# Expert loop of a transformer kernel: one split of both units of a load in place of two

## The reference

```python
def swiglu(h, w_gate, w_up, w_down):
    return (jax.nn.silu(h @ w_gate) * (h @ w_up)) @ w_down

def moe_swiglu(h, router, w_gate, w_up, w_down):
    ...
    probs = jax.nn.softmax((ht @ router).astype(jnp.float32), axis=-1)
    vals, idx = lax.top_k(probs, TOP_K)
    wts = vals / jnp.sum(vals, axis=-1, keepdims=True)
    gates = jnp.einsum('tk,tke->te', wts, jax.nn.one_hot(idx, N_EXPERTS, dtype=jnp.float32)).astype(h.dtype)
    for e in range(N_EXPERTS):
        out = out + gates[:, e:e + 1] * swiglu(ht, w_gate[e], w_up[e], w_down[e])
    return out.reshape(bsz, seq, d)
```

## Time and profile before

| what | us |
|---|---|
| median of 3 runs | 1398.68 |
| lowest, highest | 1397.64, 1400.05 |
| the profiled execution | 1395.94 |
| its span, first to last instruction | 1393.9 |
| TensorE busy in the span | 1306.4 |
| VectorE busy | 1045.1 |
| ScalarE busy | 864.5 |

### The profile page before, as it was taken

The page is one execution under the profiler, slowest core; times in us unless marked ns, Lnnn a source line. Parts: engine busy times, 40 slices in busy tenths (PEclk is TensorE's granted clock), DMA queues, the critical chain, the costliest instruction groups (busy, mean ns, idle before and its releaser), DMA issues.

```text
span 1393.9 us, 18776 instructions
## 1 busy us (share of the span) xinstructions
PE 1306.4 (94%) x6058; PEld 1067.9 (77%) x6058; DVE 1045.1 (75%) x1471; ACT 864.5 (62%) x1272; POOL 38.9 (3%) x54
## 2 busy tenths in 40 slices
PE   7999999997678999999999999999997975999998
PEld 5878888886556788888888888888886744888887
DVE  4576555565765999999999999999995856555554
ACT  4655444455644687878787878878784544444443
POOL 0000000000300000000000000000000111000000
PEclk9999999998898999999999999999998997999999
DMA  9635555554004597979798888889894410445540
GB/s 359 218 147 199 190 185 181 182 180 151 31 10 172 207 377 303 379 295 382 299 380 327 354 331 344 329 347 366 319 375 157 168 44 1 136 185 193 181 151 31
DMA packets 46121, 319.31 MB, mean 229 GB/s; under 512 B 5152, under 2 KB 6304, under 8 KB 7808
## 3 DMA queue, kind: packets, MB, share of 16 engines
q1 hardware_dynamic: 44288, 316.40, 60.1%
q10 hardware_dynamic: 1680, 2.10, 0.5%
q0 software_dynamic: 112, 0.26, 0.1%
HBM read 316.64 MB, written 2.10 MB: 229 GB/s over the span
## 4 chain that ended last, share of the span: by engine, by line
PE 81%; DVE 11%; issue 3%; ACT 2%; POOL 1%; DMA 1%; DVEq 0%; SPq 0%; ACTq 0%; POOLq 0%
PE bank L349 24%; PE bank L351 24%; PE bank L350 24%; PE bank L645 3%; DVE wl L1231 2%; PE bank L413 2%; DVE x L1645 2%; PE bank L385 1%; DMA fixed<-fixed_dram 1%; PE bank L751 1%; PE bank L580 0%; PE bank L772 0%; PE bank L664 0%; PE bank L665 0%; DVE xtl L1251 0%
## 5 line engine op out<-in xcount | busy, mean ns | idle before, releaser
L1231 DVE TENSOR_TENSOR wl<-raw,wh 128x1024 fp32r<-128x1024 f32 x598 | 714.8, 1221 | 206.0 <-ACT wh L835 194.3
L835 ACT ACTIVATE wh<-raw 128x1024 fp32r<-128x1024 f32 x598 | 631.5, 1061 | 323.1 <-PE bank L351 316.2
L349 PE MATMUL bank<-wh,xth 128*128 128x512 f32 (+2 forms) x1170 | 463.4, 396 | 12.9 <-DVE wl L1231 5.1
L351 PE MATMUL bank<-wh,xtl 128*128 128x512 f32 (+2 forms) x1170 | 454.6, 389 | 0.0
L350 PE MATMUL bank<-wl,xth 128*128 128x512 f32 (+2 forms) x1170 | 454.5, 388 | 0.0
L349 PEld LDWEIGHTS bank<-wh,xth 128*128 128x128 f32 x1170 | 221.5, 189 | 57.8 <-issue 5.3
L351 PEld LDWEIGHTS bank<-wh,xtl 128*128 128x128 f32 x1170 | 221.2, 189 | 46.0
L350 PEld LDWEIGHTS bank<-wl,xth 128*128 128x128 f32 x1170 | 221.8, 190 | 42.3
L349 PE MATMUL bank<-wh,hth 128*128 128x512 f32 x456 | 178.6, 392 | 0.0
L351 PE MATMUL bank<-wh,htl 128*128 128x512 f32 x456 | 178.0, 390 | 0.0
L350 PE MATMUL bank<-wl,hth 128*128 128x512 f32 x456 | 177.4, 389 | 0.0
(11 more groups left out here) (275 smaller groups left out, 794.2 us busy)
## 6 DMA issues: line engine op xcount, KB each, us to landing
raw<-weights_dram SPq DMA_DIRECT2D x299, 1024.0 KB, 4.9
x<-x_dram SPq DMA_DIRECT2D x1, 1024.0 KB, 7.9
bias_scratch<-act ACTq DMA_DIRECT2D x1, 1024.0 KB, 16.0
wide<-bias_scratch ACTq DMA_DIRECT2D x8, 128.0 KB, 2.2
out_dram<-x SPq DMA_DIRECT2D x4, 256.0 KB, 2.1
fixed<-fixed_dram SPq DMA_DIRECT2D x1, 600.0 KB, 8.9
rows<-rows_dram POOLq DMA_DIRECT2D x1, 256.0 KB, 6.3
cols<-cols_dram SPq DMA_DIRECT2D x1, 73.0 KB, 8.6
```

Of the source, the lines that this page charges most:

```text
L349: mm(o, lh, wh[:, wi, sl], start=start, stop=False)
L351: return mm(o, ll, wh[:, wi, sl], start=False, stop=stop)
L835: A(wh[:, c % SPLIT, :], raw[:, (c // 2) % RAW, (c % 2) * UNIT:(c % 2 + 1) * UNIT], ACT.Copy).then_inc(hi_done, 1)
L1231: V.tensor_tensor(wl[:, c % SPLIT, :], raw[:, (c // 2) % RAW, (c % 2) * UNIT:(c % 2 + 1) * UNIT], f32(wh[:, c % SPLIT, :]), ALU.subtract). ...
```

## The change

In the expert loop alone (`nt` is 1 there, and 2 in the dense layers, which keep the old functions) `follow` and `followed` are replaced by `follow_pairs` and `followed_pairs` on ScalarE and on VectorE. One instruction splits both units of a load, 2048 columns. ScalarE's waits until both slots are free, and `followed_pairs` does n - 2 units ahead of its step and 2 behind, where `followed` did n - 1 and 1. The number of slots, the loads and TensorE's program stay as they were. In the diff the lines of ScalarE are shown, and of VectorE those that differ from them; its `ffn` has the same replacements.

```diff
+            def split_hi_pair(c, i):
+
+                sc.wait_ge(raw_full[(c // 2) % RAW], 16 * (c // ROUND + 1) + 16 * i)
+                sc.wait_ge(unit_used, c - SPLIT + 2 + ROUND * i)
+                A(wh[:, c % SPLIT:c % SPLIT + 2, :], raw[:, (c // 2) % RAW, :].rearrange("p (u n) -> p u n", u=2), ACT.Copy)\
+                    .then_inc(hi_done, 2)
+
+            def follow_pairs(c, n, i):
+
+                for u in range(c, c + n, 2):
+                    split_hi_pair(u + SPLIT, i)
+
+            def followed_pairs(c, n, i, step):
+
+                follow_pairs(c, n - 2, i)
+                sc.wait_ge(unit_used, c + n + ROUND * i)
+                step()
+                follow_pairs(c + n - 2, 2, i)
+
...
             def ffn(tag, c0, nf, U, loops, width, nd, i0, f0=0, nt=NT, early=None, late=None, done=0, leave=None):
                 nj = width // P
+                some, most = (follow, followed) if nt == NT else (follow_pairs, followed_pairs)
...
-                followed(c0, ug, i0, lambda: evac(0, fb))
+                most(c0, ug, i0, lambda: evac(0, fb))
...
-                    followed(c0 + ug, ug, i0, lambda: evac(1, fb))
-                follow(c0 + 2 * ug, nd, i0)
+                    most(c0 + ug, ug, i0, lambda: evac(1, fb))
+                some(c0 + 2 * ug, nd, i0)
...
-                        followed(c + s * (ug + nd), ug, ii, lambda: evac(2 + s, fb + it * U))
-                        follow(c + s * (ug + nd) + ug, nd, ii)
+                        most(c + s * (ug + nd), ug, ii, lambda: evac(2 + s, fb + it * U))
+                        some(c + s * (ug + nd) + ug, nd, ii)
                         turned(2 + s, fb + it * U)
...
                 if late:
                     late[0]()
-                    followed(c, nd, i0, late[1])
+                    most(c, nd, i0, late[1])
...
+            def split_lo_pair(c, i):
+                dv.wait_ge(hi_done, c + 2 + ROUND * i)
+                V.tensor_tensor(wl[:, c % SPLIT:c % SPLIT + 2, :], raw[:, (c // 2) % RAW, :].rearrange("p (u n) -> p u n", u=2),
+                                f32(wh[:, c % SPLIT:c % SPLIT + 2, :]), ALU.subtract).then_inc(lo_done, 2)
+
+            def follow_pairs(c, n, i):
+                for u in range(c, c + n, 2):
+                    split_lo_pair(u + SPLIT, i)
+
+            def followed_pairs(c, n, i, step):
+
+                follow_pairs(c, n - 2, i)
+                step()
+                follow_pairs(c + n - 2, 2, i)
+
```

More of the change, by code:

```diff
@@ L900, in ffn @@
                 fb = nf * f0
-                followed(c0, ug, i0, lambda: evac(0, fb))
+                most(c0, ug, i0, lambda: evac(0, fb))
                 if nt == NT:
-                    follow(c0 + ug, 2, 0)
+                    some(c0 + ug, 2, 0)
                     turned(0, fb)
-                    followed(c0 + ug + 2, 2, 0, lambda: evac(1, fb, 6))
+                    most(c0 + ug + 2, 2, 0, lambda: evac(1, fb, 6))
                 else:
@@ L920, in ffn @@
                 for f in range(2 + loops * U, nf):
-                    followed(c, ug, i0, lambda: evac(f, fb))
+                    most(c, ug, i0, lambda: evac(f, fb))
                     if nt == NT and f == nf - 1:
                         turned(f, fb, True)
-                        follow(c + ug, nd, i0)
+                        some(c + ug, nd, i0)
                     else:
-                        follow(c + ug, nd, i0)
+                        some(c + ug, nd, i0)
                         turned(f, fb)
```

## The result

The changed kernel takes 1426.24 us (median of 4 runs, 1423.73 to 1427.65) against 1399.37 us before (4 runs, 1397.64 to 1402.27): a ratio of 1.0186, 95% interval 1.0171 to 1.0202. Run again beside 20 runs of the kernel before on another occasion it took 1425.34 against 1400.76 us, 1.0186 (1.0164 to 1.0208). The forecast was 1413.2 us, with a range of 1403 to 1430.

A forecast was written before the change was run, and what follows sets the result against it. TensorE was taken to set the pace, so the change could mainly lose cover. 8 x 1.09 + 7 x 0.55 + 1.90 = 14.5 us on 1398.68 gave 1413.2 us, range 1403 to 1430.

The forecast's parts named there:

- What bounds it: Expert loop: TensorE sets the pace in a steady stage; the change can gain little and can lose cover.
- Prices: Time of one pair split: 1.91 us on ScalarE, 2.28 us on VectorE.
- Late: End of an expert: the pair delays htl for the down product behind the gather, 1.09 us in each of 8 experts.
- Early: Start of the next expert: hbuf's first turn waits 0.69 us more; 0.55 us net, counted for 7 experts.
- End of the loop: Behind the last expert: the last additions to x wait behind the last pair, 1.90 us once.
- Steady stage: Stages within an expert: cover ahead of hbuf's turn shrinks from 0.73 to 0.18 us but holds, so cost nothing.
- longer steady stages: Expert loop: steady stages were to stay at 8.4 us; if they lengthen, the forecast is wrong.
- the dearer case: Rival, pairs at twice the single price: steady stages 0.19 us short, 1432 us in all; chance of 1421 and more 0.18.
- the dear ones: Upper end of the pair prices, twice the single: 2.12 us on ScalarE, 2.44 us on VectorE.
- The faster one: Rival: VectorE's relief removes TensorE's waits at the turns, 8 x 0.55 = 4.4 us, giving 1394.3 us; chance 0.05.
- the no-change rival: Rival: late pair behind the gather costs under 0.3 us an expert, less the 4.4 us gain; about 1398; chance 0.06.
- the forecast proper: Whole kernel: a time of 1407 to 1421 us, given chance 0.60.

The follow-up runs named there:

- e8: Changed kernel with ScalarE's program put back to singles in the old order, VectorE still in pairs: period 73.88 us, ratio 1.0007 to the kernel before.
- e9: Changed kernel with ScalarE's old program and the turned hbuf written ahead of the last splits on both engines: period 73.56 us, ratio 1.0006 to the kernel before.
- e2: Changed kernel with the turned hbuf written ahead of the last pair in every second stage, on both engines: period 75.35 us, ratio 1.0069 to the kernel before.
- e1: Changed kernel with the old order of single splits around an expert's outputs, on both engines: period 76.02 us, ratio 1.0117 to the kernel before.
- e5: Changed kernel in its pairs' order, but every unit split singly on both engines: period 73.97 us, ratio 1.0023 to the kernel before.
- e6: Changed kernel with the six stages of the inner loop written out as one pass: period 75.84 us, ratio 1.0108 to the kernel before.
- e7: Kernel before, singles on both engines, with the inner loop's six stages written out as one pass: period 73.71 us, ratio 0.9997.
- e4: Changed kernel in its pairs' order, ScalarE in pairs but VectorE splitting singly: period 76.62 us, ratio 1.0137 to the kernel before.

## Why the forecast was right in sign and short in size

- **What bounds it.** Right. TensorE sets the pace, VectorE's relief was worth next to nothing (e8, e9), and cover was what could be lost.
- **Prices.** 1.91 and 2.28 us forecast, 1.917 and 2.289 measured.
- **Late.** Forecast 1.09 us an expert, measured 1.13 (4.62 - 3.49), and e2 took 1.0 of it away. Over 8 experts 9.0 us.
- **Early.** Forecast 0.55 us net, measured 0.65: 0.79 more at the first turn, 0.11 more in the up product behind it, 0.25 less at the down product and the second turn. Over 7 experts 4.6 us. The forecast named the missing split ahead of the outputs; e1 gives it half, the pair ahead of the evacuation has the other. The first expert, which the forecast left out here, gained: its period is 0.35 us shorter, for 1.1 us at its first turn come from the new order (e5).
- **End of the loop.** Forecast 1.90 us, measured 3.2 - 1.13 = 2.1 us, and e1 took 2.0.
- **Steady stage: the step that failed.** It said "cost nothing at these prices", with 0.18 us of cover left. Measured: 2.66 - 1.13 - 0.65 = 0.88 us an expert, 6 us over 7. Two parts of it were missing from the sum. The cover was smaller than its terms: ScalarE's pair started 3.10 us into the stage (790.38 less 787.28) instead of 3.01, VectorE followed ScalarE's end by 0.10 us (790.38 + 1.92 to 792.40) instead of 0.03, the two splits took 0.02 us more, and the transposes started 0.08 us behind hbuf (795.48 to 795.56) instead of 0.05. That is 0.21 us more than the terms, against 0.18 us of cover, and the turn is 0.03 us longer. Why ScalarE's pair starts later stays open. The larger part comes behind it: once the turn waits at all, the branch at the end of a pass shows with 0.27 us, twice an expert, and the last turn, ahead of the gather, takes 0.42 us instead of 0.22. Six turns at 0.03, two at 0.27 and 0.17 at the last make the 0.88 us. e6 removed the two, e7 shows that the branch was free before; the last one's share stayed in e6. I had priced falling short of the cover by the shortfall alone, and I had named longer steady stages as a sign of being wrong.
- **Behind the loop.** Not in the forecast: 2.5 to 5.1 us that go with the granted clock, which also moves from run to run of one kernel.
- **The rivals.** The steady shortfall of the dearer case happened at the likely prices, not at the dear ones. The faster one is out by e9: even with the late cost gone, the period falls by 0.13 us, not 0.55. The numbers of the no-change rival (8 x 0.3 less 4.4 us) give 1396.7 us and not 1398.
- **The range.** It held in part by luck. 1426 us lies above the 1421 to which the forecast proper went, in the part that was kept for dearer prices; the prices came out as forecast, and a steady cost and the clock filled it.

Of the two rules of the Trainium skill (Perfetto Trace Analysis, Optimizing Scalar/DVE Operations) the one on breaking instructions up gives the outcome: e5 differs from the changed kernel only in that, and won back 2.4 of 2.66 us. Its condition, engines that are not saturated, is not what decided: VectorE was 95% busy, the case that the rule on grouping is for.

## What to carry to other kernels

Joining two instructions saves the fixed part of one (here about 0.08 us of 2.3 where they follow back to back) and delays whatever waits for the first half, or stands behind it, by a whole instruction on each engine of the chain; count the cover at every hand-over, not the busy time. A cover like the 0.18 us here, summed from half a dozen terms each known to some 0.05 us, is no cover; and when the engine that sets the pace begins to wait, add what was hidden until then, such as a loop's branch. If the joining is worth having, keep the feeding engine in singles and in its old order, and write what another engine waits for ahead of the long instruction.

## What was not expected of the hardware

- The branch of the inner loop costs TensorE nothing where hbuf was ready ahead of the turn (e7: 73.71 against 73.69 us) and 0.27 us where the last instruction of the pass had to wait (0.44 against 0.17 us at the turn, e6).
- VectorE starts a split of 2048 columns 0.10 us after ScalarE's end where it starts one of 1024 columns after 0.03. It is 0.10 too in e8, where ScalarE's instruction is a single (747.05 + 1.06 to 748.21), and 0.03 in e4, where ScalarE has the pair and VectorE singles. So it goes with VectorE's longer instruction; the cause stays open.
- The stretches at the lower clock behind the expert loop vary in one and the same kernel: 22.7 and 38.6 us in two profiles of the kernel before, and the second took 4.7 us longer.
